# Experts of a two-layer hybrid network: five of eight up blocks in three passes, another order for the last items, output copies on ScalarE

## What is computed

```python
def hier_moe(xn, w_grp, b_grp, w_exp, b_exp, w1, w3, w2):
    ...
    gate = jnp.sum(jax.nn.one_hot(eid, N_EXPERTS, dtype=jnp.float32) * w_tok[..., None], axis=1)
    hid = jax.nn.silu(jnp.einsum('td,edf->tef', t, w1)) * jnp.einsum('td,edf->tef', t, w3)
    hid = hid * gate[..., None].astype(hid.dtype)
    y = hid.reshape(t.shape[0], N_EXPERTS * EXP_FF) @ w2.reshape(N_EXPERTS * EXP_FF, dm)
```

## Time and profile before

| what | value |
|---|---|
| median of 3 runs | 1217.92 us (1217.58 to 1219.41) |
| the profiled execution's own time | 1217.04 us |
| its span, first to last instruction | 1215.3 us |
| granted TensorE clock, mean | 0.988 |
| busy: PE, DVE, ACT, POOL | 97%, 59%, 49%, 30% |
| experts of layer 0, first up product to last addition | 415.3 to 604.1 us |
| experts of layer 1, the same | 1024.2 to 1212.2 us |

### The profile page before, as it was taken

One profiled execution on the slowest core, in us unless ns is written; L12 is line 12 of the kernel. 1 busy time (PEld: TensorE's weight loads), 2 busy tenths in 40 slices (PEclk: granted clock), 3 DMA queues, 4 the chain that ended last, 5 costly groups with the idle time before them and its releaser, 6 DMA issues.

```text
span 1215.3 us, 15456 instructions
## 1 busy us (share of the span) xinstructions
PE 1173.7 (97%) x5272; PEld 869.2 (72%) x5272; DVE 719.7 (59%) x1281; ACT 590.3 (49%) x1134; POOL 361.1 (30%) x320
## 2 busy tenths in 40 slices
PE   8999999999999899999899999989999998999996
PEld 5467876788777566666678887768887775666665
DVE  4797533322422688888745992772223236888887
ACT  2733246455634266655535364453456342666661
POOL 2034440564222011113136664263342220111130
PEclk9999999999999999999999999999999999999999
DMA  9432231277102799997232230012322018999963
GB/s 294 141 139 78 32 114 70 93 293 306 70 1 95 308 404 380 389 379 283 76 130 78 70 117 23 2 70 74 134 70 70 1 70 322 394 374 393 377 237 126
DMA packets 77643, 214.92 MB, mean 177 GB/s; under 512 B 23620, under 2 KB 24560, under 8 KB 65272
## 3 DMA queue, kind: packets, MB, share of 16 engines
q1 hardware_dynamic: 64688, 180.22, 40.0%
q0 software_dynamic: 10048, 28.92, 6.5%
q10 hardware_dynamic: 2840, 4.91, 1.1%
HBM read 187.90 MB, written 32.51 MB: 181 GB/s over the span
## 4 chain that ended last, share of the span: by engine, by line
PE 85%; DVE 7%; ACT 2%; DMA 2%; issue 2%; SPq 1%; DVEq 0%; ACTq 0%
PE bank L853 40%; PE bank L1212 7%; PE bank L1245 7%; PE bank L1217 6%; PE bank L1073 2%; PE bank L1095 2%; PE bank L891 2%; PE bank L826 2%; PE bank L1154 1%; PE bank L1201 1%; PE bank L1122 1%; PE bank L1034 1%; PE bank L1268 1%; SPq L611 1%; DVE h L2491 1%
## 5 line engine op out<-in xcount | busy, mean ns | idle before, releaser
L684 POOL TENSOR_TENSOR wlo<-W,whi 128x512 fp32r<-128x512 f32 x176 | 256.3, 1468 | 444.4 <-ACT whi L1477 426.3
L1477 ACT ACTIVATE whi<-W 128x512 fp32r<-128x512 f32 x176 | 108.1, 631 | 243.8 <-PE bank L853 225.6
L853 PE MATMUL bank<-whi,xTr 128*128 128x512 f32 x480 | 193.4, 403 | 0.9 <-ACT E L1941 0.7
L853 PE MATMUL bank<-wlo,xTr 128*128 128x512 f32 x416 | 162.9, 391 | 0.0
L853 PEld LDWEIGHTS bank<-whi,xTr 128*128 128x128 f32 x480 | 90.8, 189 | 21.8 <-POOL wlo L684 1.7
L853 PE MATMUL bank<-whi,E4r 128*128 128x512 f32 x256 | 99.8, 390 | 0.0
L1217 PE MATMUL bank<-E4r,E1r 128*128 128x512 f32 x360 | 98.5, 422 | 0.0
L1245 PE MATMUL bank<-whi,E2r 128*128 128x512 f32 x256 | 89.3, 410 | 7.4 <-DVE E2r L2452 5.9
L853 PEld LDWEIGHTS bank<-wlo,xTr 128*128 128x128 f32 x416 | 78.7, 189 | 16.6 <-issue 1.2
L2043 DVE TENSOR_TENSOR h<-bank,h 128x512 f32<-128x512 f32 x32 | 21.8, 692 | 115.0 <-PE bank L853 115.0
L1217 PEld LDWEIGHTS bank<-E4r,E1r 128*128 128x128 f32 x360 | 67.6, 188 | 27.0 <-issue 7.4
(11 more groups left out here) (498 smaller groups left out, 2422.7 us busy)
## 6 DMA issues: line engine op xcount, KB each, us to landing
E<-in_moe_w SPq DMA_DIRECT2D x48, 1024.0 KB, 11.5
W<-in_moe_w SPq DMA_DIRECT2D x32, 1024.0 KB, 9.7
xT<-in_moe_w SPq DMA_DIRECT2D x16, 1024.0 KB, 14.3
W<-in_od_w_in SPq DMA_DIRECT2D x7, 2048.0 KB, 8.4
ybuf<-E SPq DMA_DIRECT2D x26, 512.0 KB, 8.1
ybuf<-memV POOLq DMA_DIRECT2D x12, 1024.0 KB, 19.9
W<-in_w_mem_kv SPq DMA_DIRECT2D x4, 2048.0 KB, 9.3
W<-in_xa_wq SPq DMA_DIRECT2D x4, 2048.0 KB, 7.8
```

What stands on the lines that cost most here:

```text
L684: pool.tensor_tensor(wlo[s_ % RING][:, :], slot(name)[:, block_of(name, k), :], whi[s_ % RING][:, :].bitcast(F32), ALU.subtract).then_inc( ...
L853: ins = pe.matmul(bank(u + t)[:, :], a, b, start=(k == 0 and n == 0), stop=(k == KT - 1 and n == 2))
L1477: act.activation(whi[s_ % RING][:, :], slot(name)[:, block_of(name, k), :], ACT.Copy).then_inc(S["w_hi"], 1)
```

## The change

It has four parts. SPLIT becomes 5: three up blocks stay whole and five are made in passes; the fifth high and low parts get room in `E5r` and `smr`, the counts of parts and of `up_used` follow. Both halves of an item's output are copied by ACT, and DVE's `output` goes. In the last quad, item 3's w2 parts go into the buffers of the up parts (`end_whi`, `end_wlo`) and not into the ring. And the order of the last quad changes on PE, ACT and DVE, with the one-hots made one by one and the additions of `add_row` and of the banks interleaved.

```diff
-        xg_hi, xg_lo = v3(E1r, 4, 3072, 3584), v3(E1r, 4, 2560, 3072)
-        SPLIT = 4
-        up_hi = [E4r[:, 512 * c:512 * c + 512] for c in range(SPLIT)]
-        up_lo = [E4r[:, 2048 + 512 * c:2560 + 512 * c] for c in range(SPLIT)]
+        SPLIT = 5
+        xg_hi, xg_lo = v3(E1r, SPLIT, 3072, 3072 + SPLIT * P), v3(E1r, SPLIT, 3072 - SPLIT * P, 3072)
+        up_hi = [E4r[:, 512 * c:512 * c + 512] for c in range(4)] + [E5r[:, 4096:4608]]
+        up_lo = [E4r[:, 2048 + 512 * c:2560 + 512 * c] for c in range(4)] + [smr[:, 0:512]]
...
+        end_whi, end_wlo = up_hi[0:4], up_lo[0:4]
...
                     turn_hidden(q, 2, last=True)
-                    down(q, 2, late=1)
                     pe.wait_ge(S["late_onehots"], l + 1)
                     pe.wait_ge(m["xt_ready"], q * (2 * SLOTS) + 2 * SLOTS)
                     to_tokens(0, 0)
                     pe.wait_ge(m["hid_ready"], q * SLOTS + 3)
                     to_tokens(0, 1)
+                    down(q, 2, late=1)
                     turn_hidden(q, 3, last=True)
+                    down(q, 3, late=2)
                     to_tokens(1, 0)
                     to_tokens(1, 1)
-                    down(q, 3, late=2)
-                    for n in range(2):
-                        to_tokens(n, 2)
-                    for t in range(3):
-                        to_tokens(2, t)
+                    to_tokens(0, 2)
+                    to_tokens(1, 2)
+                    to_tokens(2, 0)
+                    to_tokens(2, 1)
+                    to_tokens(2, 2)
                     for n in range(3):
                         to_tokens(n, 3)
...
-                    act.wait_ge(m["y_filled1"], q * SLOTS + (j + 1))
-                    act.activation(yo[par][:, 512:1024], banks[6][:, :], ACT.Copy).then_inc(m["y_ready1"], 1)
+                    for half in range(2):
+                        act.wait_ge(m[f"y_filled{half}"], q * SLOTS + (j + 1))
+                        act.activation(yo[par][:, half * 512:(half + 1) * 512], banks[5 + half][:, :], ACT.Copy)\
+                           .then_inc(m[f"y_ready{half}"], 1)
...
                 item(last_quad, 0)
-                for n in range(LATE):
-                    item(last_quad, SLOTS - LATE + n, late=n)
+                item(last_quad, 1, late=True)
+                gated_hidden(last_quad, 2)
+                down_high(last_quad, 2, [w[:, :] for w in whi])
+                gated_hidden(last_quad, 3)
+                hidden_high(last_quad, 2)
+                down_high(last_quad, 3, end_whi)
+                late_high(last_quad, 2, 1)
+                hidden_high(last_quad, 3)
+                late_high(last_quad, 3, 2)
```

More of the change, by code:

```diff
@@ L1242, in down @@
                             xh, xl = hThi[par][:, k * P:(k + 1) * P], hTlo[par][:, k * P:(k + 1) * P]
[L1243 removed]
+                            wh, wl = (end_whi, end_wlo) if late == LATE - 1 else (whi, wlo)
+                            wh, wl = wh[2 * half + k], wl[2 * half + k]
                             for n, (a, b) in enumerate(((xh, wh), (xh, wl), (xl, wh))):
@@ L1777, in rows_high, with gated_hidden, down_high @@
                     act.activation(xg_hi, xgT[:, KT - SPLIT:KT, :], ACT.Copy).then_inc(m["hi_parts"], 1)
-                def item(q, j, late=None):
-                    par = j % 2
-                    last = late is not None and j > 1
+                def gated_hidden(q, j):
                     act.wait_ge(m["hid_filled"], q * SLOTS + (j + 1))
-                    act.activation(silu[par], banks[2 + par][:, 0:FF], ACT.Silu).then_inc(m["silu_ready"], 1)
+                    act.activation(silu[j % 2], banks[2 + j % 2][:, 0:FF], ACT.Silu).then_inc(m["silu_ready"], 1)
+                def down_high(q, j, dst):
                     act.wait_ge(m[f"w2_{j}"], q * 16 + 16)
@@ L1787, in item, with hidden_high @@
                         for k in range(2):
-                            act.activation(whi[2 * half + k][:, :], w2s[j][:, k, half * 512:(half + 1) * 512], ACT.Copy)\
+                            act.activation(dst[2 * half + k], w2s[j][:, k, half * 512:(half + 1) * 512], ACT.Copy)\
                                .then_inc(m["hi_parts"], 1)
-                    if not last:
-                        up_high(q, j + 2, 0, 2)
+                def hidden_high(q, j):
                     act.wait_ge(m["ht_filled"], q * SLOTS + (j + 1))
-                    act.activation(hThi[par], banks[4][:, 0:2 * P], ACT.Copy).then_inc(m["hi_parts"], 1)
@@ L1794, in item @@
-                    if not last:
-                        up_high(q, j + 2, 2, SPLIT)
-                        rows_high(q, j + 2)
-                    if late is not None:
-                        act.wait_ge(S["late_cols"], 2 * l + 1)
-                        if late == LATE - 1:
-                            act.wait_ge(m["y_stored0"], q * (8 * SLOTS) + 16)
-                        for half in range(2):
-                            act.wait_ge(m[f"y_filled{half}"], q * SLOTS + (j + 1))
-                            act.activation(late_hi[late][:, half * 512:(half + 1) * 512], banks[5 + half][:, :], ACT.Copy,
-                                           scale=late_gate[:, late:late + 1]).then_inc(S["late_hi"], 1)
+                    act.activation(hThi[j % 2], banks[4][:, 0:2 * P], ACT.Copy).then_inc(m["hi_parts"], 1)
@@ new lines, in late_high @@
+                def late_high(q, j, n):
+                    act.wait_ge(S["late_cols"], 2 * l + 1)
+                    if n == LATE - 1:
+                        act.wait_ge(m["y_stored0"], q * (8 * SLOTS) + 16)
+                    for half in range(2):
+                        act.wait_ge(m[f"y_filled{half}"], q * SLOTS + (j + 1))
+                        act.activation(late_hi[n][:, half * 512:(half + 1) * 512], banks[5 + half][:, :], ACT.Copy,
+                                       scale=late_gate[:, n:n + 1]).then_inc(S["late_hi"], 1)
@@ L1805, in item @@
+                def item(q, j, late=False):
+                    par = j % 2
+                    gated_hidden(q, j)
+                    down_high(q, j, [w[:, :] for w in whi])
+                    up_high(q, j + 2, 0, 2)
+                    hidden_high(q, j)
+                    up_high(q, j + 2, 2, SPLIT)
+                    rows_high(q, j + 2)
+                    if late:
+                        late_high(q, j, 0)
                         return
@@ L2439, in rows_low, with down_low @@
                     tt(xg_lo, xgT[:, KT - SPLIT:KT, :], xg_hi.bitcast(F32), ALU.subtract).then_inc(m["lo_parts"], 1)
-                def low_parts(q, j, last=False):
+                def down_low(q, j, high, low, last=False):
                     for half in range(2):
@@ L2491, in add_row, with add_late @@
                     v(stt(h[:, t, :], Yg[j][:, t, :], gate[:, j, t:t + 1], h[:, t, :], ALU.mult, ALU.add))
+                def add_late(t):
+                    dve.wait_ge(S["late_filled"], TT * l + t + 1)
+                    for half, b in enumerate(token_banks[t]):
+                        hs = h[:, t, half * 512:(half + 1) * 512]
+                        ins = tt(hs, banks[b][:, :], hs, ALU.add)
+                    ins.then_inc(m["h_combined"], 1)
                 def last_turn(q):
```

72 lines of the change are left out of this document (29 added, 43 removed).

## The result

| | before | after |
|---|---|---|
| median of 5 runs each, side by side | 1217.92 us (1217.21 to 1223.47) | 1207.16 us (1205.39 to 1209.97) |
| ratio, 95% interval | | 0.9903 (0.9881 to 0.9924) |
| the profiled execution's own time, its span | 1217.04, 1215.3 us | 1207.16, 1205.4 us |
| compared again, with the experiments | 1217.47 us (20 runs) | 1210.67 us (10 runs), ratio 0.9939 (0.9917 to 0.9962) |

The change makes the kernel faster, by 1.0% in the first comparison and 0.6% in the second; all fifteen runs of it together have a median of 1209.5 us.

A forecast was written before the change was run, and what follows sets the result against it. PE's own work was taken to bound the expert loops, with DVE's queue at their starts and ends. The terms 2.1 - 4.6 - 2.0 - 3.1 + 1.1 + 0.8 = -5.7 us took 1217.9 to 1212.2; range 1209.2 to 1216.6.

The forecast's parts named there:

- Steady item: Item of both expert layers' loops: 0.18 us less PE work, 10.34 to 10.17 us; 26 x 0.177 = -4.6 us.
- the sum: Whole kernel: 2.1 - 4.6 - 2.0 - 3.1 + 1.1 + 0.8 = -5.7 us.
- rivals 3, 4 and 5: Loop: 3, transfers hold items at 10.34 us, 0.07; 4, blocks get no cheaper, 0.06; 5, ACT becomes the clock, slower, 0.05.
- First item: First item of each layer: PE's passes wait for DVE's low parts and rows; +1.06 us per layer, +2.1.
- Last items of layer 1: End of layer 1's experts: PE's stall moves from down(2) to down(3), DVE's additions end last; -2.0 us.
- the replay: Last items in the new order, replayed with rows' durations from the last up's start; DVE ends at 30.5 us.
- +0.8 for a new half-clock stretch: Half-clock stretch after the 1.8 us stall ahead of down(3): two equal outcomes, 0 and 1.6 us, taken as 0.8.
- Last items of layer 0: End of layer 0's experts: earlier hand-over to the next norm's transposes, -3.1 us, with +1.1 for the clock.
- rival 2: Last items of both layers give nothing, as DVE's in-order tail or late y gathers eat it; -2.5 us, 1215.4; chance 0.12.
- What remains is the same: Everything outside the experts' loops, first items and last items keeps its time; no term in the sum.
- Rival 4: Up blocks in the loop get no cheaper in passes, +0.03 us a block; about -0.4 us, 1217.5; chance 0.06.
- +1.1 for layer 0: Half-clock stretch from PE's wait, 24.9 to 28.0, for the third tile in layer 0's last items; 1.1 us.

The follow-up runs named there:

- e8: The kernel after, with each layer's first item keeping four whole-precision blocks and four in passes; 1207.99 us, ratio to before 0.9926.
- e4: The kernel before, with four unused products added ahead of PE's wait near 811 us in the mixer; 1217.12 us, ratio 0.9997.
- e7: The kernel after, with one row addition of the last items moved on DVE ahead of the first pair of late additions; 1207.36 us, ratio to before 0.9932.
- a1: The kernel after, unedited, profiled a second time and timed again; 1210.67 us, ratio to before 0.9939.
- e0_before_again: The kernel before, unedited, profiled a second time and timed again; 1218.45 us, ratio 0.9992.

## Why the prediction was right and wrong
- **Steady item: right.** 10.17 forecast; the profiles of kernels with five blocks in passes show 10.17 to 10.21, those with four 10.34 to 10.37. The saving per item depends on the pair of profiles: 0.135 us in the first, 0.13 to 0.21 over the four pairings of two profiles each, where the sum had 0.177. In the first pair the loops gave 3.5 us and not 4.6. ACT and the transfers (99% of the queues' time, 389 GB/s) were no bound: rivals 3, 4 and 5 fell. The Trainium skill's bound of about 358 GB/s for transfers between HBM and SBUF ("DMA: Bandwidth & Descriptors", section "Where 436 GB/s comes from") was passed here too, by these 389 GB/s. They count the stores to `ybuf` as well, so they are not a rate of loads alone, as my prediction read them.
- **First item: right.** +1.06 forecast, +1.05 and +1.03 measured; PE's wait 1.6 forecast, 1.50 measured. The wait's releaser is the rows' low part on DVE, and with one low part less e8 has its first items back at 10.92 and 10.90.
- **Last items of layer 1: right in the path, with a slip in the clock.** -2.0 forecast and -1.86 measured; DVE's last addition ends 30.6 us after the last up began, where the replay had 30.5. The +0.8 for a new half-clock stretch did not come. Every sign of the replay came: no idle ahead of down(2), 1.68 ahead of down(3) where 1.8 was forecast, none before the last tile products, DVE without a gap, PE done 5.7 us before it. The half-clock stretch of the earlier trace rows is gone; the only one in these items begins at 1199.8, when PE has ended. That is part of the gain: e4, the kernel before but for its fillers in the mixer, had no stretch there and took 34.55 us, 1.0 less than the first profile.
- **Last items of layer 0: right on the first pair, too small in general.** -3.1 + 1.1 forecast, -1.75 measured against the first profile. But that profile was one in which the last store landed in 2.7 us. In four of six profiles with the old order it took 6.6 to 7.1, DVE stood 1.4 to 2.1 us, and the last items took 37.2 to 39.7. The new order leaves one row addition ahead of down(2)'s low part and puts the others behind it, so that a late store is hidden in most cases: the kernel after had one of 7.7 us, DVE stood 0.61 us and PE not at all ahead of down(2). Late gathers were rival 2's reason for a smaller gain; here they are a reason for a larger one.
- **The step that failed is "What remains is the same".** It took the rest of one profiled execution for a constant. Outside the experts the first pair of profiles differ by 4.3 us in the mixer and attention of layer 1 and 0.6 at the start, and the second profiles of both kernels show the values the other way round (414.37 before, 416.77 after). In the sum this was a term of zero that had to be one of zero with a width of some 4 us. In the first comparison it went for the change, by luck, and the median, which is the profiled execution itself, fell 2 us below the range. Without these 4.9 us it would have been 1212.0, at the forecast, which is in part chance too: the experts gave 0.7 us less than the sum, and the sum started 0.9 above the profiled execution of before.
- **The second weakness is the parts' independence.** The sum added the split's loop gain and the tail's gain. By themselves the split gave 0.03% (nothing clear of noise), the order 0.45%, the copies a loss of 0.24%; together they gave 0.6 to 1.0%. In the old order the split's longer queue on DVE costs PE 0.8 to 0.9 us in each layer's last items, which takes what was left of its loop gain; in the new order that wait is gone. The forecast, for the whole change, did not need this; a forecast for the split alone did.
- **Slips that moved little.** The saving of a block is worked out as 0.18 and used as 0.177; by its own terms, 3.46 / 4 - 0.68, it is 0.185, 0.2 us over all items. Rival 4's terms add to about -0.1 and not -0.4. The chances of faster, same and slower should be 0.78, 0.17 and 0.05 by the rivals' own numbers.
- **The clock.** The sum had +1.1 for layer 0 and +0.8 for the 1.8 us stall. The one in layer 0 came in both profiles of the change (3.4 and 6.8 us at half clock), the other in neither. In e7 PE stood 2.94 us at the same place in layer 0 and no stretch followed.

## What to carry to other kernels
Take two or three profiles of the kernel before when the effect is below 1%: where stretches at half clock lie and whether a store lands in 2.7 or 7 us differed between executions by more than most terms of the sum. When a loop gets shorter, look at what the code behind it waits for that doesn't get shorter with it (here DVE's queue, which the split made longer, and a store to memory), and move what doesn't depend on it ahead; test parts in combination, since each alone can come out at nothing.

## What was not expected of the hardware
- The same transfer has two landing times in otherwise equal executions: the panel `out10` 7.7 to 7.9 us in six of the fourteen profiles and 9.0 to 9.4 in the rest, the last store to `ybuf` of layer 0 2.7 to 3.1 us in three of them and 6.5 to 8.6 in the rest. Both values come with either kernel.
- Half-clock stretches near 811 us came in some profiles and not in others after nearly the same waits of PE: with 3.72 us of idle before the transposes in the kernel before and 3.65 in a1 (6.8 us each), with 2.33 in e0_before_again 3.4 us, with 2.22 in the kernel after none.
- The steady item has more than one pace for one program, 10.34 and 10.37 before, 10.17 and 10.21 after, at a full clock in all four. What sets it was not found.
